# Norm turns between two projections: six units by token halves, one program block, three tiles in PSUM

## The reference

```
def adaln_norm(x, c, g, w_ada, b_ada):
    mod = jax.nn.silu(c) @ w_ada + b_ada
    shift, scale, gate = jnp.split(mod, 3, axis=-1)
    h = rms_norm(x, g) * (1.0 + scale[:, None, :]) + shift[:, None, :]
    return h, gate[:, None, :]
...
    x = x + gate * y            # y = mixer(h) ends in "@ w_out"
...
def rms_norm(x, g):
    y = xf * lax.rsqrt(jnp.mean(xf * xf, axis=-1, keepdims=True) + NORM_EPS)
```

## Time and profile before

| | us |
|---|---|
| Median of 3 runs (2247.63 to 2254.78) | 2248.76 |
| The profiled execution | 2251.47 |
| its span | 2249.3 |
| PE busy | 2183.9 (97%) |
| DVE busy | 1561.1 (69%) |
| POOL busy | 1242.5 (55%) |
| ACT busy | 921.0 (41%) |

### The profile page before, as it was taken

One profiled execution on the slowest core, in us unless ns is written; L12 is line 12 of the kernel. 1 busy time (PEld: TensorE's weight loads), 2 busy tenths in 40 slices (PEclk: granted clock), 3 DMA queues, 4 the chain that ended last, 5 costly groups with the idle time before them and its releaser, 6 DMA issues.

```text
span 2249.3 us, 32224 instructions
## 1 busy us (share of the span) xinstructions
PE 2183.9 (97%) x11911; PEld 1953.7 (87%) x11911; DVE 1561.1 (69%) x3031; ACT 921.0 (41%) x1513; POOL 1242.5 (55%) x670
## 2 busy tenths in 40 slices
PE   6999999999999999999999999999999999999999
PEld 6897989888888877888999999999998888888887
DVE  5726777575455656442899999999984667776665
ACT  3235576332455424431334333555553333333332
POOL 1624222375213341232588788766657777787875
PEclk9999999999999999999999999999999999999999
DMA  7253424222221441233478788999989999999995
GB/s 281 87 178 113 141 91 136 83 93 95 88 83 66 137 145 38 75 105 130 135 259 286 264 293 270 341 356 333 356 294 342 360 356 335 367 356 363 352 359 218
DMA packets 164475, 492.41 MB, mean 219 GB/s; under 512 B 15072, under 2 KB 64608, under 8 KB 162912
## 3 DMA queue, kind: packets, MB, share of 16 engines
q1 hardware_dynamic: 107872, 305.79, 39.6%
q0 software_dynamic: 36864, 134.23, 16.0%
q10 hardware_dynamic: 19584, 50.34, 5.9%
HBM read 437.87 MB, written 52.43 MB: 218 GB/s over the span
## 4 chain that ended last, share of the span: by engine, by line
PE 40%; DVE 8%; POOL 2%; DMA 1%; issue 1%; ACT 0%; DVEq 0%; ACTq 0%; POOLq 0%
PE ps L2472 22%; PE ps L2436 14%; PE ps L2454 4%; POOL t_split L2581 1%; DVE arena L2700 1%; DVE arena L2669 1%; DVE arena L2660 1%; DVE arena L2661 1%; DVE norm_rows L2638 1%; DVE rope L2638 1%; DVE arena L2665 1%; DVE arena L2695 1%; DVE arena L2638 1%; DVE arena L2656 1%; DVE arena L2703 0%
## 5 line engine op out<-in xcount | busy, mean ns | idle before, releaser
L2581 POOL TENSOR_TENSOR t_split<-t_raw,t_split 128x1024 fp32r<-128x1024 f32 x225 | 550.3, 2447 | 211.3 <-ACT t_split L2507 208.3
L262 POOL TENSOR_TENSOR w_split<-ring,w_split 128x1024 fp32r<-128x1024 f32 x113 | 271.4, 2403 | 509.8 <-ACT w_split L254 464.0
L2436 PE MATMUL ps<-h_hi,t_split 128*128 128x384 f32 x2048 | 537.2, 338 | 5.2 <-ACT e_gel L2513 3.0
L2472 PE MATMUL ps<-t_split,w_split 128*128 128x512 f32 x2304 | 523.1, 389 | 3.3 <-DVE t_split L2755 1.8
L2472 PEld LDWEIGHTS ps<-t_split,w_split 128*128 128x128 f32 x2304 | 432.2, 188 | 94.0 <-DVE t_split L2755 2.2
L286 PE MATMUL ps<-h_hi,w_split 128*128 128x512 f32 x1328 | 417.6, 392 | 0.0
L2507 ACT ACTIVATE t_split<-t_raw 128x1024 fp32r<-128x1024 f32 x256 | 270.3, 1057 | 339.6 <-PE ps L2472 241.3
L2436 PEld LDWEIGHTS ps<-h_hi,t_split 128*128 128x128 f32 x2048 | 373.7, 189 | 7.4 <-POOL t_split L2581 3.9
L2436 PE MATMUL ps<-h_lo,t_split 128*128 128x384 f32 x1024 | 344.0, 336 | 0.0
L286 PEld LDWEIGHTS ps<-h_hi,w_split 128*128 128x128 f32 x1328 | 249.3, 188 | 52.6 <-issue 0.7
L286 PE MATMUL ps<-h_lo,w_split 128*128 128x512 f32 x664 | 258.4, 389 | 0.0
(11 more groups left out here) (354 smaller groups left out, 3273.2 us busy)
## 6 DMA issues: line engine op xcount, KB each, us to landing
ring<-w_stream SPq DMA_DIRECT2D x203, 512.0 KB, 3.4
t_raw<-u_table SPq DMA_DIRECT2D x128, 512.0 KB
t_raw<-v_table SPq DMA_DIRECT2D x128, 512.0 KB
gelu_scratch<-e_gel ACTq DMA_DIRECT2D x128, 192.0 KB
gates_scratch<-arena ACTq DMA_DIRECT2D x8, 3072.0 KB
arena<-gelu_scratch SPq DMA_DIRECT2D x32, 768.0 KB, 6.4
arena<-gates_scratch SPq DMA_DIRECT2D x32, 768.0 KB
first<-w_stream SPq DMA_DIRECT2D x16, 512.0 KB, 15.5
```

Of the source, the lines that this page charges most:

```text
L262: pool.tensor_tensor(w_split[:, i % RS, 1, :], ring[:, n % R, :], w_split[:, i % RS, 0, :].bitcast(F32), ALU.subtract).then_inc(lo_done, 1)
L2436: mm = pe.matmul(ps[:, 6 + n % 2, 0:NT], t_split[:, n % RAWS, u, k * P:(k + 1) * P], h_parts[h][:, k, P:T], start=(k + u + h == 0), stop=( ...
L2472: mm = pe.matmul(ps[:, 2 * i + half, :], w_split[:, b % 2, w, at:at + P], t_split[:, m % RAWS, v, half * 512:(half + 1) * 512], start=(n + ...
L2581: pool.tensor_tensor(t_split[:, m % RAWS, 1, :], t_raw[:, m % RAWS, :], t_split[:, m % RAWS, 0, :].bitcast(F32), ALU.subtract).then_inc(t_ ...
```

## The change

`TurnNorm` takes the place of `ColumnNorm` in the three turns. The last three units of the output projection (5, 6, 7) and the first three of the next are each made in two halves of 256 tokens, 24 products of 256 columns per half. The order on TensorE is: first halves of 5, 6, 7; second halves of 5, 6, 7 with the sums and the spread of the first half's norm inside units 5 and 6; then the new units on the first token half, with the second half's sums and spread between them; then the new units on the second token half. Squares, totals, chain, scale, upper and lower part are all done by halves. For the first token half the scaled tiles 0, 1 and 2 are written to PSUM (banks 0 to 2) and not to SBUF. The last square goes into the total too, so that the sums are two products per half and set. The filler products are gone, and both projections stand in one program block. In n2 the products that spread the gains' factor come after the group. The cast of the next projection's pieces 0 and 1 moves behind the root of the first half.

The core of the diff (declarations, and the re-indented code of the joined blocks, are left out):

```diff
+        HALVES = (slice(0, T // 2), slice(T // 2, T))
+        BY_HALF, EARLY, IN_BANKS = 5, 4, 3
...
+        def half_unit(pe, w, bank, src, half, ks, ready=None):
+            at = HALVES[half]
+            for k in ks:
+                if ready:
+                    ready.wait(pe, half * KD + k + 1)
+                for a, b in HI_LO:
+                    mm = pe.matmul(ps[:, bank, at], w[:, a, k * P:(k + 1) * P], src[b][:, k, at],
...
+            def pe_sums(self, pe, half):
+                self.totaled.wait(pe, turn_of(KD - 1, half) * self.sets)
...
+            def scaled_at(self, half, k):
+                if half == 0 and k < IN_BANKS:
+                    return ps[:, k, HALVES[half]]
+                return ntmp[:, k, HALVES[half]]
...
+            def pe_second(self, pe, pieces, banks):
+                first, last = range(0, KD // 2), range(KD // 2, KD)
+                w = [piece_ready(pe, pieces[0])]
+                half_unit(pe, w[0], banks[0], h_parts, 0, first, self.done)
+                self.pe_sums(pe, 1)
+                w.append(piece_ready(pe, pieces[1]))
+                half_unit(pe, w[1], banks[1], h_parts, 0, first, self.done)
+                half_unit(pe, w[0], banks[0], h_parts, 0, last, self.done)
+                self.pe_spread(pe, 1)
+                half_unit(pe, w[1], banks[1], h_parts, 0, last, self.done)
+                w.append(piece_ready(pe, pieces[2]))
+                half_unit(pe, w[2], banks[2], h_parts, 0, range(KD), self.done)
+                half_unit(pe, w[0], banks[0], h_parts, 1, first, self.done)
...
+            def act_second(self, act, piece, added_x):
+                self.act_square(act, KD - 1, 1, added_x)
+                self.act_upper(act, 0, EARLY)
+                split_hi(act, piece)
+                self.act_upper(act, 0, EARLY + 1)
+                self.act_root(act, 1)
...
+            def dve_second(self, dve, add_last):
+                add_last(dve)
+                self.dve_scale(dve, 0, EARLY)
+                self.dve_total(dve, KD - 1, 1)
+                self.dve_scale(dve, 0, EARLY + 1)
+                self.dve_lower(dve, 0, EARLY)
+                self.dve_lower(dve, 0, EARLY + 1)
+                def between():
+                    for k in range(EARLY + 2, KD):
+                        self.dve_scale(dve, 0, k)
+                self.dve_chain(dve, 1, between)
...
+                for u in range(BY_HALF, KD):
+                    added_x.wait(pe, u - 2)
+                    w[u] = piece_ready(pe, at + u)
+                    half_unit(pe, w[u], 4 + u % 3, h_parts, 0, range(KD)).then_inc(half_used.sem, 1)
+                for u in range(BY_HALF, KD):
+                    added_x.wait(pe, turn_of(u, 0) + 1)
+                    half_unit(pe, w[u], 4 + u % 3, h_parts, 1, range(KD // 2))
+                    if u == BY_HALF:
+                        norm.pe_sums(pe, 0)
+                    if u == BY_HALF + 1:
+                        norm.pe_spread(pe, 0)
+                    half_unit(pe, w[u], 4 + u % 3, h_parts, 1, range(KD // 2, KD)).then_inc(piece_used, 1)
...
-                keep_busy(pe, 3, 5)
-                n1.pe_spread(pe)
-                keep_busy(pe, 3, 7)
-                feature_group(pe, units6[0:3], (0, 1, 2), h_parts, n1.done)
+                n1.pe_second(pe, units6[0:3], (0, 1, 2))
```

More of the change, by code:

```diff
@@ L1423, in out_projection, with add_x @@
                            pool_before=None, split_before=0, split_upto=3, order=range(KD), between=None, following=()):
-            added_x = since("added_x", KD)
+            added_x = since("added_x", TURNS)
+            half_used = since("half_used", KD - BY_HALF)
+            def add_x(dve, u, half):
+                tokens = turn_tokens(u, half)
+                if u >= BY_HALF and half == 0:
+                    half_used.wait(dve, u - BY_HALF + 1)
+                else:
+                    dve.wait_ge(piece_used, used_of(at + u + 1))
+                dve.scalar_tensor_tensor(out=xT[:, u, tokens], in0=ps[:, 4 + u % 3, tokens],
+                                         scalar=gate_cols[:, u:u + 1], in1=xT[:, u, tokens],
+                                         op0=ALU.mult, op1=ALU.add).then_inc(added_x.sem, 1)
             @block.sync
@@ L1556, in build @@
-        share = orders[:, 2 * P + 2 * TT:]
-        with phase() as block:
+            qd, vd = area(0, 8, T), area(4096, TT, D)
+            kd_pad = place("kd_pad", 8192, [2, KD, T])
+            zd = area(16384, 8, T)
+            raw6 = area(16384, 4, T)
+            rt61 = area(18432, 2, T)
+            vt6 = area(19456, 2, T)
+            Z_FIRST, Z_LAST = 24, 31
+            v_turned, v_taken = sem("v_turned"), sem("v_taken")
+            order6 = ["act"] * 32
+            ev6 = {who: since("evacuated_" + who, order6.count(who)) for who in ("dve", "act")}
@@ new lines, in build, with class_major, by_class, roped_to @@
+            left6 = evacuated(order6, ev6)
+            units6 = [n for name in ("dq", "dk", "dv", "dz") for n in PIECES[name]]
+            BY_TILE = 3
+            def class_major(u, x):
+                return x if u < BY_TILE else x.rearrange("p (r a) -> p a r", r=TT)
+            def by_class(u, x):
+                return x if u < BY_TILE else x.rearrange("p (a r) -> p a r", r=TT)
+            def roped_to(r, half=None):
+                if r < 8:
+                    return class_major(r, qd[:, r, :])
+                return class_major(r - 8, kd_pad[half * DH:(half + 1) * DH, half, r - 8, :])
@@ new lines, in build @@
+            rope_dil = rope_direct(16, lambda r: raw6[:, r % 4, :], rt61, roped_to,
+                                   lambda r: r % 4, left6, lambda r, x: by_class(r % 8, x), halved=8)
+            pad_zeroed = since("pad_zero", 8)
+            ada_sum6 = norm_rows[:, 0:2, :].rearrange("p (one a) b -> p one (a b)", one=1)
+            mod_taken = sem("mod_taken")
+            pos_i, ang, turns = area(23040, T).bitcast(I32), zd[:, 4, :], area(18944, 2, T)
+            pos_loaded = sem("pos_loaded")
@@ L1925, in build @@
-        units9 = [n for name in ("q2", "k2", "v2", "cc", "cu", "cb") for n in PIECES[name]]
-        ada_sum9 = area(19200, 2, PIECE)
-        sine_done = since('added_x', 2)
-        with phase() as block:
+            raw9, sq9, qn9 = area(0, 5, T), area(2560, 5, T), area(5120, 5, T)
+            qr9 = area(7680, 5, T)
+            v9 = area(10240, TT, P)
+            ccs = area(10752, 4, T)
+            hp = area(12800, 4, T + 2)
+            conv = area(14856, 4, T)
+            rt91, rt92 = area(16904, 2, T), area(17928, 2, T)
@@ L1929, in _ @@
+            ada_sum9 = area(19200, 2, PIECE)
+            sine_done = since('added_x', 2)
             @block.sync
```

363 lines of the change are left out of this document (219 added, 144 removed).

## The result

| | kernel before | changed kernel |
|---|---|---|
| median, us | 2254.40 (2247.63 to 2256.55, 8 runs) | 2260.09 (2255.50 to 2268.05, 8 runs) |
| ratio of the changed kernel to before | | 1.0039, 95% interval 1.0022 to 1.0056 |
| profiled execution: time / span, us | 2251.47 / 2249.3 | 2264.51 / 2262.7 |

The changed kernel is slower by 8.8 us (5.0 to 12.6), by the ratio; the two medians alone stand 5.7 us apart. Differences between whole times are the ratio's from here on. The forecast was +3.5 us, with "within 0.3%" as the likeliest of the three outcomes (faster, the same, slower); 0.39% is beyond that, on the slow side. The +8.8 us lies inside the stated range, which reached up to +12.2 (2261 on a kernel of 2248.76), at two and a half times the forecast.

A forecast was written before the change was run, and what follows sets the result against it. TensorE, busy 97%, was taken as the bound, with 32.75 us in three gaps. Turns +0.6, +1.4 and 0.0, loads +0.2, clock +1.3 made +3.5 us on 2248.76: 2252, range 2240 to 2261.

The forecast's parts named there:

- Unit prices: On TensorE a 256-column product costs 0.120 us, so a turn's products add 1.9 us; VectorE and ScalarE halves priced likewise.
- Rival 3: On TensorE, half products cost as much as 304-column ones: +16 us, 2267; chance 0.03.
- The wait that decides: VectorE instructions with two SBUF inputs stand until GpSimd's running split ends; if only totals stood, 6 us less in all.
- Rival 1: The VectorE/GpSimd port never bites at halves, so the turns' waits shrink: about 2241; chance 0.21.
- 40 to 46 us for turn 1: Stretch from unit 5 to the group's end in the first turn; outside these bounds the forecast is wrong.
- rival 4: Halves overlap better than the chain of dependences allows, with all waits gone: 2230; chance 0.03.
- The walk through the turns: Step-by-step times of the three turns: first 42.5 us (+0.6), second 47.7 (+1.4), third 0.0 against before.
- The wait before tile 5: TensorE idles 1.7 us before tile 5 in the first turn, as its lower part meets GpSimd's split.
- The clock: One 3.4 us stretch at 1.2 GHz on dense work behind the turns' late waits: +1.3 us.
- rival 2: All three turns fall to 1.2 GHz inside dense work, two for 6.7 us: 8.4 more, 2259; chance 0.22.
- The step that failed: Behind turn two, late gains delay weight loads, but the weights hold; only an existing 0.87 us stall grows, +0.2 us.

The follow-up runs named there:

- cast_behind: Changed kernel with the cast of the group's third unit one place back on ScalarE, behind tile 5's upper part, in each turn: 1.0017 of the kernel before.
- no_banks: Changed kernel with the three early tiles in SBUF, not in PSUM: 1.0049 of the kernel before, +11.0 us.
- Act_order: Changed kernel, gains still late, with unit 3's copy and square and unit 5's copy and root ahead of the waiting weight casts on ScalarE: 1.0029 of the kernel before.
- Gain_early: Changed kernel with turn two's four gain-spread products straight behind the second half's spread, not behind the group: 1.0030 of the kernel before.
- gain_late: Kernel before, no halves, with only the gains' four spread products moved behind the group of three units: ratio 1.0024, +5.4 us.
- after_filled: Changed kernel with filler products added in the waits before tile 2 and before the second sums of each turn: 1.0043 of the kernel before, +9.7 us.

## Why the prediction was wrong

**Unit prices: right.** 0.120 us a half product; 0.48 for a half on VectorE, 0.42 a total and a square, 0.505 an upper part. Rival 3 is out.

**The wait that decides: right.** Tile 5's lower part at 2.30 (expected near 2.3), totals at 1.58 and 1.45, PSUM inputs exempt; cast_behind and no_banks each turned it by moving one thing. Rival 1 and rival 4 are out: 40 to 46 us for turn 1 were the bounds, 42.63 the result. The exclusive lock of the Trainium skill (SBUF — State Buffer, section SBUF: two separate sides) agrees with these numbers.

**The walk through the turns: right to 0.2 us.** Turn 1 was put at 42.5 and took 42.63. Turn 2 was put at 47.7 and took 49.30 with 3.4 us at 1.2 GHz in dense work, 1.7 us: 47.6 without. This closeness is partly luck: tile 6 began 28.4 us into turn 1 and 32.7 into turn 2, where the walk has 27.95 and 31.8, and what follows was shorter by about as much. Turn 3 was put at 42.5 and took 44.42, where turn 1's same code took 42.63; its slow stretch reaches 4.1 us beyond the last wait (985.7 to 989.8), which is 2.0 us. The wait before tile 5 that was to show didn't: slow products filled it.

**The clock: mechanism right, size too small.** I put in one slow stretch, +1.3. Two turns of three lost time to it, 1.7 and 1.8 us; a third stretch stood behind the stall at 801.63. That is 2.2 us over the term within the turns, and it is part of rival 2, whose three turns and 8.4 us were too many. Rival 2's total, +10.6, is nearer to the +8.8 than my own, but by luck: half of the loss lay behind turn 2, where it had none. The Trainium skill (TensorE: Matmul & The Clock Gate, section Terms) puts the penalty at the slow time times one less the granted share, one half here. By the trace that is right only for what lies beyond the last wait: turn 1's 3.4 us cost nothing, where by that rule they would cost 1.7, and the 10.2 us of turn 3 cost 1.8 against 5.1.

**The step that failed: "the seventh unit's weights are split at 781.5 and wanted at 783, so the loads hold; only the existing stall of 0.87 at 793.76 grows, +0.2".** It measured +5.26. That the gains are 8 us late, that eight pieces stand behind them and that the loads wait for their slots, was all in the text. That the weights hold came true, though at other times: in the changed kernel the seventh unit's were split at 787.1 and first used at 793.2. I compared the weights with the moment at which TensorE wants them, and stopped. I did not name what is queued behind the waiting cast on ScalarE: the copy and square of unit 3 (1.48 us of stall), the copy of unit 5 and the root of the q-norm (1.85 more), and I did not ask what the clock makes of a stall of 2.7 us (1.7). Act_order settles it: the same late loads, with those instructions ahead of the cast, cost 0.4 us. Gain_early and gain_late settle that the late spread starts it. The sum of the forecast with this term at 5.26 and the clock at 3.5 would be 0.6 + 0.0 + 1.4 + 5.3 + 3.5 = 10.8, against 10.5 found in the four stretches and 8.8 (5.0 to 12.6) in the times.

It stays open what sets the length of a slow stretch: 3.4 us in turn 1 and 10.2 in turn 3 of the changed kernel, with the same waits, and 10.2 in both of no_banks.

## What to carry to other kernels

When an edit makes a load late, don't stop at when its data are wanted: write down the instructions that stand behind the one that waits for it, on its own engine, and who waits for those. Four spread products put behind a group cost as much (5.3 us) as the three halved turns together (5.2); moving them and one cast turned +8.8 us into -4.3. And where a gap is broken into many small waits, look for the clock to fall inside the dense work behind them, as it did here; short waits with filler in the rest kept it up, filler with the long waits left empty brought nothing.

## What the runs showed of the hardware

- A stretch at 1.2 GHz is free as long as TensorE has a wait ahead of it that it would have spent anyway (443.7 to 447.1 in turn 1: the turn took 42.63 with it and 42.65 in after_filled without it). In gain_late such a stretch ahead of a stall made the stall 1.7 us shorter, 1.01 against 2.72.
- The five kernels with late gains and the old order on ScalarE have a slow stretch within the 60 us behind turn 2; the four with early gains, the two with turn 2 as before, and act_order with its one stall of 1.13 us have none.
- A VectorE instruction with two SBUF inputs stands until the split beside it ends, and the next one goes at once: a pair of lower parts took 1.90 in place of 0.88 us. With one input in PSUM it took 0.47 in the middle of a split.
